# A residual MLP up projection computed as seven products of weight and token quarters, with the sums of weights added in flight by accumulating DMAs

## What is computed

```python
xn2 = rmsnorm(x, norm2_g[l])                      # x: 512 tokens x 1024
x = x + jnp.square(jax.nn.relu(xn2 @ w_up[l])) @ w_down[l]   # w_up: 1024 x 4096
```

## Time and profile before

| | |
|---|---|
| median of 3 runs | 1969.29 us (1969.24 to 1969.61) |
| span of the profiled execution, first to last instruction | 1967.4 us |
| what lies around the span (median less span) | 1.9 us |
| TensorE busy (PE) | 1959.2 us, 100% of the span |
| VectorE (DVE), ScalarE (ACT), GpSimd (POOL) busy | 1024.1, 764.9, 83.8 us |
| mean granted TensorE clock | 0.999 of full speed |
| the two halves of the MLP, up and down | 4 stretches of 87 us, 348 us in all |

### The profile page before, as it was taken

The page is one execution under the profiler, slowest core; times in us unless marked ns, Lnnn a source line. Parts: engine busy times, 40 slices in busy tenths (PEclk is TensorE's granted clock), DMA queues, the critical chain, the costliest instruction groups (busy, mean ns, idle before and its releaser), DMA issues.

```text
span 1967.4 us, 23153 instructions
## 1 busy us (share of the span) xinstructions
PE 1959.2 (100%) x9686; PEld 1614.8 (82%) x9686; DVE 1024.1 (52%) x1394; ACT 764.9 (39%) x1226; POOL 83.8 (4%) x132
## 2 busy tenths in 40 slices
PE   9999999999999999999999999999999999999998
PEld 8888888888888888888888888888888888887776
DVE  5553466435453436643334355545554447596675
ACT  5556563332323333442134232222222321447864
POOL 0000000000000000000000000000000000005541
PEclk9999999999999999999999999999999999999999
DMA  6222222223122242233233323232323334521011
GB/s 214 84 68 85 65 86 75 86 91 106 65 91 86 87 148 86 86 107 108 86 105 89 106 86 107 86 107 89 105 86 107 86 124 114 152 81 44 23 55 65
DMA packets 184295, 183.36 MB, mean 93 GB/s; under 512 B 5120, under 2 KB 159232, under 8 KB 184192
## 3 DMA queue, kind: packets, MB, share of 16 engines
q1 hardware_dynamic: 179840, 172.15, 28.2%
q10 hardware_dynamic: 4352, 9.75, 1.6%
HBM read 175.59 MB, written 4.19 MB: 91 GB/s over the span
## 4 chain that ended last, share of the span: by engine, by line
PE 98%; ACT 1%; DVE 0%; DMA 0%; issue 0%; POOL 0%; DVEq 0%; ACTq 0%
PE bank L1403 85%; PE bank L1630 2%; PE bank L1611 2%; PE bank L1644 2%; PE bank L1501 1%; PE bank L1490 1%; PE bank L1529 1%; PE bank L1413 1%; ACT raw L1663 0%; PE bank L1464 0%; PE bank L1433 0%; PE bank L1509 0%; PE bank L1577 0%; PE bank L1446 0%; PE bank L1620 0%; PE bank L1431 0%
## 5 line engine op out<-in xcount | busy, mean ns | idle before, releaser
L1403 PE MATMUL bank<-xh,wh 128*128 128x512 f32 x1352 | 534.1, 395 | 0.0
L1403 PE MATMUL bank<-xh,wl 128*128 128x512 f32 x1352 | 527.6, 390 | 0.0
L1403 PE MATMUL bank<-xl,wh 128*128 128x512 f32 x1352 | 527.0, 390 | 0.0
L1680 ACT CAST wh<-raw 128x2048 fp32r<-128x2048 f32 (+2 forms) x151 | 279.5, 1854 | 408.8 <-PE bank L1403 405.1
L2234 DVE TENSOR_TENSOR wl<-raw,wh 128x2048 fp32r<-128x2048 f32 (+2 forms) x151 | 335.0, 2221 | 169.5 <-ACT wh L1680 169.3
L1403 PEld LDWEIGHTS bank<-xh,wl 128*128 128x128 f32 x1352 | 253.4, 187 | 53.8
L1403 PEld LDWEIGHTS bank<-xh,wh 128*128 128x128 f32 x1352 | 253.7, 188 | 50.3
L1403 PEld LDWEIGHTS bank<-xl,wh 128*128 128x128 f32 x1352 | 253.8, 188 | 50.0
L1403 PE MATMUL bank<-wh,xh 128*128 128x512 f32 x320 | 129.4, 404 | 0.0
L1403 PE MATMUL bank<-wh,xl 128*128 128x512 f32 x320 | 125.1, 391 | 0.0
L1403 PE MATMUL bank<-wl,xh 128*128 128x512 f32 x320 | 125.1, 391 | 0.0
(11 more groups left out here) (325 smaller groups left out, 2925.8 us busy)
## 6 DMA issues: line engine op xcount, KB each, us to landing
raw<-in_w_in SPq DMA_DIRECT2D x49, 1024.0 KB, 5.0
raw<-in_a_w_in SPq DMA_DIRECT2D x32, 1024.0 KB, 5.5
raw<-in_w_up SPq DMA_DIRECT2D x16, 1024.0 KB, 5.3
raw<-in_w_down SPq DMA_DIRECT2D x16, 1024.0 KB, 5.8
raw<-in_w_proj_b SPq DMA_DIRECT2D x8, 1024.0 KB, 5.1
raw<-in_a_w_out SPq DMA_DIRECT2D x8, 1024.0 KB, 5.7
raw<-in_w_out SPq DMA_DIRECT2D x4, 1024.0 KB, 5.2
raw<-in_w_kv SPq DMA_DIRECT2D x4, 1024.0 KB, 4.9
```

Source lines behind the costliest of these rows:

```text
L1403: m = e.matmul(o, p, q, start=k == 0 and n == 0, stop=k == K - 1 and n == 2)
L1680: m = e.copy(hi, r)
```

## The change

The up projection of each quarter of the hidden width (group g = 0..3 of each half f; 512 hidden features, two column halves of 256) is taken as a 2x2 block product. The weight block has four quarters: A and C (first column half, feature rows 0-511 and 512-1023), B and D (second column half). The tokens are cut in two halves of 256, so the activations have four quarters too. Instead of eight quarter products seven are made, with sums of quarters as operands, and combined into four output pieces "11", "12", "21", "22" (Winograd's form of Strassen's method).

- A product (`seven`) is 2 x 4 steps of 3 matmuls with 256 columns: 24 matmuls. There are 2 x 4 x 7 = 56 of them, in the hand-written order `SEVENS`.
- The weight operands are A, A+B, A+B+D, A+B+C+D, B+D, C and D. SyncE loads each quarter (0.5 MB, in runs of 1 KB) into half a `raw` buffer; GpSimd then issues DMAs that read another quarter from HBM and add it to the one in SBUF (`sum_weights`, at most three under way). There are five sums in each group, 40 in all. A sum waits until the weights before it in its buffer have been split.
- Each product's weights are cast by ACT and subtracted by DVE in 128 x 1024 pieces (`part`); there are four such half buffers, so a part can be made when the product four before it has been read.
- Sums of activation quarters are made once, beside w_out's tiles: in `wo` on DVE, with casts on ACT and low parts in `low`, into `xh`/`xl` and the new `xeh`/`xel`.
- Products 1, 6, 5 and 3 of a group accumulate in one PSUM bank. After 1, 6 and 5 ACT copies the bank to SBUF (`shot`), and the next of them waits for that copy. `piece` on DVE adds bank and copy (not for "12") and applies relu and scale, `piece` on ACT squares and casts, `piece_low` on DVE subtracts. `piece_low` comes one product later than its piece, behind that product's `part`.
- The two matmuls and the root for the token scale stand behind the third product.
- Some semaphores are shared under one name; elsewhere the order is as before.

```diff
+SEVENS = [(0, 1), (1, 1), (0, 2), (0, 7), (0, 6), (1, 2), (0, 5), (1, 7), (0, 3), (0, 4),
+          (1, 6), (2, 1), (1, 5), (2, 2), (2, 7), (1, 3), (1, 4),
+          (2, 6), (3, 1), (2, 5), (3, 2), (3, 7), (3, 6), (2, 3), (3, 5), (2, 4), (3, 3), (3, 4)]
+SUM_OF = {1: ("A", 0), 7: ("A", 1), 6: ("A", 2), 3: ("A", 3), 5: ("B", 1), 2: ("C", 0), 4: ("D", 0)}
+ADDED = {("A", 1): "B", ("A", 2): "D", ("A", 3): "C", ("B", 1): "D"}
+SHOT = {1: "11", 6: "21", 5: "22"}
+PIECE_OF = {2: "11", 5: "22", 3: "12", 4: "21"}
...
+def sum_ready(g, x, step):
+
+    at = SEVENS.index
+    return at((g, 5)) - 7 if x == "B" else at((g, PRODUCT_OF[x, step - 1])) - 3
...
+    for i, (g, n) in enumerate(line):
+        while sums and (sums[0][0] <= i or i == len(line) - 1):
+            out.append(("sum_weights", f, *sums.pop(0)[1:]))
+        out.append(("seven", f, g, n))
+        if f == 0 and i == ROOT[1]:
+            out += [("sum_squares", 1), ("root", 1)]
+        if n in SHOT:
+            out.append(("shot", f, g, n))
+        if n in PIECE_OF:
+            out.append(("piece", f, g, PIECE_OF[n]))
+        out += after_chunk(("seven", f, g, n)) + low
+        low = [("piece_low", f, g, PIECE_OF[n])] if n in PIECE_OF else []
...
+        def seven(f, g, n):
...
+            w.wait_ge(*told("lo", ("seven", f, g, n)))
+            hi, lo = split_half(("seven", f, g, n))
+            for t in range(2):
+                for k in range(4):
...
+                    for x, (p, q) in enumerate(((hi, h), (hi, l), (lo, h))):
+                        m = e.matmul(bank[:, t * 256:(t + 1) * 256], p[:, c], q,
...
+        def part(f, g, n):
+            name, (x, step) = ("seven", f, g, n), SUM_OF[n]
+            if step:
+                w.wait_ge(*told(f"sum{SUMS.index((f, g, x, step)) % 3}", f, g, x, step))
...
+            for old in BEFORE[name]:
+                w.wait_ge(*told(*chunk_read(old)))
+            e.copy(split_half(name)[0], raw_half(("quarter", f, g, x))).then_inc(*tell("hi", name))
...
+        def piece(f, g, c):
+            t = shot_place(g, c)
+            w.wait_ge(*(told("st_out", f, g, c) if c == "12" else told("st_out", f, g, c, "relu")))
+            act(t[:, :], t[:, :], ACT.Square).then_inc(*tell("up_sq", f, g, c))
...
+            e.copy(h_part(hh, g, c), two(t[:, :])).then_inc(*tell("hh", f, g, c))
...
+        def sum_weights(f, g, x, step):
...
+            if (x, step - 1) in PRODUCT_OF:
+                w.wait_ge(*told("lo", ("seven", f, g, PRODUCT_OF[x, step - 1])))
+            else:
+                w.wait_ge(*told(f"half{SLOT[PLACE[name]]}", f, g, x))
+            e.dma_start(raw_half(name).rearrange("p (k c) -> p k c", k=4), rows_of(a[more[1]], *more[2:6]),
+                        accum_op=ALU.add).then_inc(*tell(f"sum{n % 3}", f, g, x, step, by=16))
```

More of the change, by code:

```diff
@@ L95, in chunk @@
     CHUNKS.append((name, matrix, r0, K, c0, C, kind))
+    if kind not in ("whole", "quarter"):
+        SPLIT.append(name)
 def col(key, name, c0, K, xs, freed):
@@ L158, in lay_out @@
     for f in range(2):
[L159 to L162, removed]
+        for x, g in QUARTER_LOADS:
+            chunk(("quarter", f, g, x), "w_up", 512 * (x in "CD"), 4, f * 2048 + g * 512 + 256 * (x in "BD"), 256,
+                  "quarter")
+        SPLIT.extend(("seven", f, g, n) for g, n in SEVENS)
         for c in range(8):
@@ L222, in after_chunk @@
 def after_chunk(name):
[L224 to L228, removed]
+    out = []
+    for new in AFTER.get(name, []):
+        if new[0] == "seven":
+            out.append(("part", *new[1:]))
+        elif new in PIECES:
+            out += [("w_piece", new, x) for x in range(4)]
+        elif name not in LATE and new not in PIECED:
+            out.append(("w", NTH[new]))
+    return out
 LATE = (("vsw", 0), ("vsw", 1))
-PIECES = (("wo", 1), ("up", 0, 2))
+PIECES = (("wo", 1),)
 PIECED = (("q", 0, 1), ("bo", 0, 0), ("bo", 0, 1), ("bo", 1, 0), ("bo", 1, 1), *PIECES)
@@ L272, in summed @@
     o = whole(key)
-    split = [t for t in o if k == 7 and t[0] in ("w", "w_piece")]
+    split = [t for t in o if k == 7 and t[0] in ("w", "w_piece", "part")]
     return [t for t in o if t not in split] + squared(s, k) + split
@@ L383, in make_order @@
     for f in range(2):
-        o += whole(("up", 1, 0, 0), ("up", 1, 0, 1)) if f else rooted(1, ("up", 0, 0, 0), ("up", 0, 0, 1))
-        o += whole(*[("up", f, c, j) for c in range(8) for j in range(2)][2:])
+        o += sevens(f)
         for k in range(8):
@@ L423, in some @@
             for x in t:
-                if x[0] == "mm" and ends_chunk(*x[1:]) and AFTER[ends_chunk(*x[1:])] in PIECED:
-                    pieces.extend(("w_piece", AFTER[ends_chunk(*x[1:])], y) for y in range(4))
+                if x[0] == "mm" and ends_chunk(*x[1:]):
+                    pieces.extend(("w_piece", new, y) for new in AFTER.get(ends_chunk(*x[1:]), ()) if new in PIECED for y in range(4))
         del fill[:n]
@@ L1383, in mm @@
                     w.wait_ge(*told("xl", 0, *x_part(b, k)))
+            elif ready == "hl":
+                for event in h_pieces(xs[1], k):
+                    w.wait_ge(*told(*event))
             else:
@@ L2904, in sync @@
             slot = SLOT[n]
-            if slot in SLOT[:n]:
-                old = CHUNKS[max(x for x in range(n) if SLOT[x] == slot)]
-                w.wait_ge(*(told("w1", *old[0][1:]) if old[6] == "whole" else told("lo", old[0], 3) if old[0] in PIECED else told("lo", old[0])))
+            for old in RAW_BEFORE[n]:
+                w.wait_ge(*told(*raw_free(old)))
             m = a[matrix]
```

393 lines of the change are left out of this document (275 added, 118 removed).

## The result

| | time, us (median) | ratio to before, 95% interval |
|---|---|---|
| before | 1969.45 (1969.24 to 1969.77) | |
| after | 2033.0 (2032.62 to 2033.09) | 1.0322 (1.0307 to 1.0337) |

The change costs 63.6 us. The forecast was 2015, in a range of 1994 to 2060. The profiled execution's span grew from 1967.4 to 2030.4 us.

A forecast was written before the change was run, and what follows sets the result against it. TensorE bounds the kernel before; in the up halves the VectorE-ScalarE pair becomes the bound. First half 109.7, second 101.7, down 182.2: 393.6 against 348.0 us, +45.6, so 2015; range 1994 to 2060, the forecast's own 1998 to 2031.

The forecast's parts named there:

- slow sums: Rival, chance 0.14: in the up halves one sum keeps GpSimd longer than 5 us; +86 us, 2055.
- Exchange: Up halves: VectorE and ScalarE, passing tiles in written order, need 24.4 us a group, 3.49 a product; TensorE needs 2.88.
- TensorE's pace: Up products: 256-column matmuls at 0.12 us each, 2.88 us a product; TensorE's own work falls by 12.7 us.
- Sums: Groups 0 and 3: product 6 follows 7 at once; sum lands in 6.5 us; two blocks, 12.2 us a half.
- Late x parts: First up half, third product: VectorE falls behind beside w_out's last tiles, and TensorE waits 4 us.
- Root and reciprocal: First up half: root (0.69) and reciprocal (3.35), before in VectorE's spare time, lengthen the chain by 4.0 us.
- Down ends: First w_down chunk's cast and subtraction stand behind late pieces: 3.1 us, and 1.0 for the last pieces; 4.1 each half.
- The renamed semaphores and moved buffers add no instruction.: Rest of the kernel: nothing else changes its cost; no time was added for it.
- The clock: Rival, chance 0.12: TensorE's some nine stops of 4 to 5 us drop it to 1.2 GHz; 21 us, 2036.
- faster: Rival, chance 0.08: the exchange does not bind, below 20.2 us a group TensorE does; 12.7 us come back, 1957.

The follow-up runs named there:

- e8_best2: The changed kernel with part casts first on ScalarE, reordered products, bank rotation restored, first w_down chunk in pieces, earlier low parts, deferred x sums: 1973.2 us.
- e6_cast_first_no_sums: The changed kernel with ScalarE's part cast ahead of the bank copy and piece work, and the sums of weights left out: 1979.8 us.

## Why the prediction was right, and where it was not

The direction and the mechanism held; the time was 18 us short. The 2033.0 us lie within 1994 to 2060, but just above the forecast's own range, which by its bounds was 1997 (written as 1998) to 2031. That the time is still inside the whole range is owed to the room left for slow sums, which did not come. By its own steps:

**Exchange, 3.49 us a product.** Right. One instance in after, VectorE's timeline and then ScalarE's:

```profile
882.20 0.68 DVE L2779 TENSOR_TENSOR tmp<-bank,tmp 128x512 f32<-128x512 f32 x1
882.92 0.69 DVE L2360 SCALAR_TENSOR_TENSOR tmp<-tmp,rs 128x512 f32<-128x512 f32 x1
885.91 1.23 DVE L2765 TENSOR_TENSOR wl<-raw,wh 128x1024 fp32r<-128x1024 f32 x1 [2.30 <-ACT wh L1856]
887.05 0.68 DVE L2786 TENSOR_TENSOR hl<-tmp,hh 128x512 fp32r<-128x512 f32 x1
```

```profile
883.64 0.63 ACT L1820 ACTIVATE tmp<-tmp 128x512 f32<-128x512 f32 x1 [2.62 <-DVE tmp L2360]
884.31 0.62 ACT L1881 CAST hh<-tmp 128x512 fp32r<-128x512 f32 x1
884.83 1.99 ACT L1856 CAST wh<-raw 128x1024 fp32r<-128x1024 f32 x2
```

From the add to the part's subtraction 3.71 us, and 1.14 more until VectorE is free: 3.71 and 1.13 were forecast. The half without sums took 91.2 us (forecast 89.5), and without the exchange 80.9. The two kernels differ by ScalarE's order alone. One reading behind this step was wrong. The 43.3 and 40.7 us of idle time are those of 740 to 1140 us, so of the whole MLP and more. They were put down to one up stretch, in which VectorE, busy 52 of 87 us, cannot be idle for 84. In that stretch the trace of before shows 20.3 us behind `hh` and 7.8 behind `wh`. The sum does not use them.

**TensorE's pace, 0.12 us.** Right: 0.1204 over 672 matmuls. The 12.7 us of less work are real and stay invisible until both bounds are gone.

**Sums, 12.2 us a half.** The size was right (12.1 and 11.7), with a landing of 7.1 us where 6.5 was chosen, the middle of two rival values, and five waits (2.0 to 7.8 us, 30.3 in all) where four were counted. That these 30.3 us of waits cost 23.8 us of time, near the 24.4 forecast, is in part luck. The count of sums was wrong. The sections above speak of five in a group and 40 in all; the trace shows 32 issues, four in a group and 16 in a half, which leaves GpSimd some 6 us for each, where an issue takes 1.46. "Slow sums" was therefore further away than it was made to look. The estimate from the Trainium skill, "DMA: Bandwidth & Descriptors", section "Anatomy of one DMA — SWDGE (gpsimd) path", was 3.2 us; neither the 7.1 with accumulation nor the 4.7 without agrees, and by it the term would have been mis-sized by half.

**Late x parts, 4.0 us.** Too small: the stop was 6.6. VectorE was behind by 4.2 us at w_out's last tile and not by 1.5. Its add of that tile, which before waited for TensorE alone, started at 815.36 before and at 819.58 after:

```profile
801.46 0.68 DVE L2704 TENSOR_TENSOR xT<-xT,bank 128x512 f32<-128x512 f32 x1
819.58 0.68 DVE L2704 TENSOR_TENSOR xT<-xT,bank 128x512 f32<-128x512 f32 x1
```

The first line is the add of the fourth tile from the end. Three tiles of 5.44 us ahead of 815.36 is 799.04, so VectorE was 2.4 us behind there already (before it was 1.8 behind at the same tile and caught up), and 1.8 more came by the last tile. The forecast had the second part and took the first as nothing. From the last add to the third product it then took 8.1 us, where 8.4 was forecast.

**Root and reciprocal, 4.0 us.** Near it by a difference, but not shown. The exchange costs 13.6 us in the first half and 10.3 in the second, 3.3 us more where the root is. The two halves also differ in their stops and in the slow matmuls behind them, and no kernel was run without the root.

**Down ends, 4.1 us each.** Mis-sized: 5.9 each. The stops were 3.5 and 4.1 us where 3.1 was forecast, and the rest of each stage took 2.4 and 1.8 us more than before where 1.0 was. In that rest stand matmuls at the lower clock: behind the second stop, from 1132.61 to 1135.60 us, seven follow at 0.43 us in place of 0.2266, and here TensorE is the bound. In the first stage there is also the 0.8 us wait in front of the next half. The bank rotation is what made the difference: with the banks restored the stops are 2.9 us, no w_down matmul follows at 0.43, and the stages took 91.1, the forecast's figure. In e8_best2, with the first chunk in pieces and the low parts early, they have before's 87.07.

**"The renamed semaphores and moved buffers add no instruction."** This sentence failed. True for instructions, it left out that a ring which loses its customers deals other banks to everyone behind. That cost 9.3 us: 6.2 behind the MLP (810.1 to 803.9) and the rest in the down stages. It is half of what the forecast missed. No row of the trace of before could show it, but the code could: 32 draws fewer from a ring of five.

**The clock.** A rival with 21 us and 0.12. The mechanism happened beside the exchange, not in its place. The section "HAM oscillation — how this bites in real kernels" of the Trainium skill's page "TensorE: Matmul & The Clock Gate" says that waits between bursts make them start cold, and the rows above agree (0.50). Its price of 21 us was not borne out: filled stops gave back 3.5 us, with 95 of 169 slow matmuls still there, since in the up halves TensorE was mostly not the bound. How much a kernel without any slow matmul would gain stays open.

The 18 us that were missing, by stage: up 0 +6.8 (of it 2.6 in the stop for x parts; the 20 matmuls behind it took 4.20 us, 1.8 more than at 0.12), up 1 +1.2, the down stages +3.6, and 6.5 behind the MLP.

**The rival "faster"** named the right point, 20.2 us for a group: in e6_cast_first_no_sums the group gets there, and the time is 1979.8, with the banks still rotated (behind the MLP 810.8 us where before took 803.6). Even without that loss the ends (first half 90.8) would have eaten the gain.

## What to carry to other kernels

Where two engines each work through a written order and pass tiles to each other, put what a third engine waits for ahead of what nobody waits for yet, on each engine by itself; here moving casts on one engine was worth 18 us with no operation added or left out. Take two suspected bounds away together as well as singly: 18.4 and 21.5 us were 53.2 together, and either result alone would have called the other bound small. And when a stage stops drawing from a shared ring, set the ring on by what it no longer draws, or a stage far behind pays.

## What the runs showed of the hardware

- An accumulating DMA of 0.5 MB issued by GpSimd landed in 7.1 us, the same without accumulation in 4.7. The issue took GpSimd 1.46 us and 0.76, the packets were 16896 and 4608 for 16.78 MB, and the loads on SyncE's queue beside it landed in 4.8 and 3.9 us.
- In e6_cast_first_no_sums 672 matmuls of 256 columns, each with a new 128x128 weight, follow at 0.1204 us over 81 us, though a weight load is recorded at 0.19 us.
- Behind stops of 3.5 to 6.6 us TensorE's granted clock was 0.50 for 4 to 5 us, with matmuls of 256 columns at 0.21. Of two stops of 1.8 us in after, the one that ended at 1114.2 was followed by 0.50 (1115.50 to 1118.80), the one that ended at 919.0 by 1.00 (919.00 to 922.00). Taking some 7 us of slow pace out of the up halves, which other engines bound, shortened them by 2.5.
